# Eight feature tiles of the second modulation's shift rows, summed on VectorE in the latent stages

## The reference, cut to what matters

```python
def modulation(cond, w, b, n):
    m = jax.nn.silu(cond) @ w[:, :n * D_MODEL] + b[:n * D_MODEL]
    return jnp.split(m, n, axis=-1)          # shift, scale, gate

for i in range(DEPTH):                       # DEPTH = 2
    sh, sc, gt = modulation(c_lat, w_ada[i], b_ada[i], 3)
    u = x * (1.0 + sc) + sh
    y = even_mixer(u @ w_in_e[j], ...) if i == 0 else odd_mixer(u @ w_in_o[j], ...)
    x = layer_norm(alpha * x + gt * y, ln_g[i], ln_b[i])
```

## Time and profile before

| what | value |
|---|---|
| median of 3 runs | 2435.35 us (2435.2 to 2438.71) |
| the profiled execution's own time | 2434.28 us |
| its span, first to last instruction | 2432.4 us |
| mean granted TensorE clock | 0.993 of full |
| PE busy | 2355.5 us (97%) |
| DVE busy | 1436.6 us (59%) |
| ACT busy | 1081.7 us (44%) |
| POOL busy | 71.0 us (3%) |
| bytes moved by DMA | 492.88 MB, mean 203 GB/s |

### The profile page before, as it was taken

How to read it: one execution, slowest core, us unless ns; L and a number is a source line. 1 busy time by engine, 2 the same in 40 slices (tenths; PEclk the granted TensorE clock), 3 DMA queues, 4 the chain that set the end, 5 groups by cost and what they waited for, 6 DMA issues and landing times.

```text
span 2432.4 us, 29720 instructions
## 1 busy us (share of the span) xinstructions
PE 2355.5 (97%) x12180; PEld 1908.0 (78%) x12180; DVE 1436.6 (59%) x1400; ACT 1081.7 (44%) x1130; POOL 71.0 (3%) x116
## 2 busy tenths in 40 slices
PE   6999999999999999999999989999999999999998
PEld 2677887887687888878778777888888888888886
DVE  2354567566937786666567785655555545545454
ACT  2223645534744444546555443455544334334333
POOL 1000001000000000000000100000000000000000
PEclk9999999999999999999999999999999999999999
DMA  9974678757865796555545213654556566565563
GB/s 338 328 266 141 196 264 273 246 173 292 332 222 195 265 350 193 208 173 179 174 140 189 81 31 105 219 178 153 170 181 189 190 191 190 190 190 186 194 208 121
DMA packets 232163, 492.88 MB, mean 203 GB/s; under 512 B 21505, under 2 KB 23617, under 8 KB 224993
## 3 DMA queue, kind: packets, MB, share of 16 engines
q1 hardware_dynamic: 219792, 435.84, 54.6%
q0 software_dynamic: 12240, 55.18, 6.1%
HBM read 485.22 MB, written 5.77 MB: 202 GB/s over the span
## 4 chain that ended last, share of the span: by engine, by line
PE 87%; DVE 7%; ACT 2%; DMA 2%; issue 2%; SPq 0%; DVEq 0%; ACTq 0%
PE banks L2878 71%; PE banks L3011 5%; PE banks L2951 2%; DMA modulation_weights<-in_w_ada 1%; PE banks L2974 1%; DVE weights_lo L1671 1%; ACT weights_hi L842 1%; PE banks L3182 1%; PE banks L3051 1%; PE banks L3382 1%; PE banks L2991 1%; DMA weights_raw<-in_w_in_e 0%; DVE decayed_a L1961 0%; PE banks L3287 0%; DVE inverse_products L2583 0%
## 5 line engine op out<-in xcount | busy, mean ns | idle before, releaser
L1671 DVE TENSOR_TENSOR weights_lo<-weights_raw,weights_hi 128x2048 fp32r<-128x2048 f32 (+1 forms) x348 | 795.1, 2285 | 768.3 <-ACT weights_hi L842 766.8
L842 ACT ACTIVATE weights_hi<-weights_raw 128x2048 fp32r<-128x2048 f32 (+1 forms) x348 | 664.8, 1911 | 984.6 <-PE banks L2878 896.4
L2878 PE MATMUL banks<-weights_hi,acts_hi 128*128 128x512 f32 (+1 forms) x2032 | 797.9, 393 | 4.5 <-DVE weights_lo L1671 4.4
L2878 PE MATMUL banks<-weights_hi,acts_lo 128*128 128x512 f32 (+1 forms) x2032 | 789.4, 388 | 0.0
L2878 PE MATMUL banks<-weights_lo,acts_hi 128*128 128x512 f32 (+1 forms) x2032 | 789.1, 388 | 0.0
L2878 PEld LDWEIGHTS banks<-weights_hi,acts_hi 128*128 128x128 f32 x2032 | 381.5, 188 | 90.9 <-issue 15.0
L2878 PEld LDWEIGHTS banks<-weights_hi,acts_lo 128*128 128x128 f32 x2032 | 381.4, 188 | 78.9
L2878 PEld LDWEIGHTS banks<-weights_lo,acts_hi 128*128 128x128 f32 x2032 | 381.6, 188 | 76.1 <-issue 0.5
L2878 PE MATMUL banks<-weights_hi,hidden_hi 128*128 128x512 f32 x320 | 125.3, 392 | 0.5 <-DVE weights_lo L1671 0.5
L2878 PE MATMUL banks<-weights_hi,hidden_lo 128*128 128x512 f32 x320 | 124.6, 389 | 0.0
L2878 PE MATMUL banks<-weights_lo,hidden_hi 128*128 128x512 f32 x320 | 124.5, 389 | 0.0
(11 more groups left out here) (599 smaller groups left out, 2314.1 us busy)
## 6 DMA issues: line engine op xcount, KB each, us to landing
weights_raw<-in_w_in_e SPq DMA_DIRECT2D x72, 1024.0 KB, 5.5
weights_raw<-in_w_up SPq DMA_DIRECT2D x64, 1024.0 KB, 5.5
weights_raw<-in_w_down SPq DMA_DIRECT2D x64, 1024.0 KB, 5.1
weights_raw<-in_w_in SPq DMA_DIRECT2D x44, 1024.0 KB, 5.1
modulation_weights<-in_w_ada SPq DMA_DIRECT2D x64, 512.0 KB, 9.6
raw_eight<-in_w_ada SPq DMA_DIRECT2D x32, 1024.0 KB, 7.6
weights_raw<-in_w_in_o SPq DMA_DIRECT2D x32, 1024.0 KB, 5.6
gate_piece<-in_w_ada POOLq DMA_DIRECT2D x32, 512.0 KB, 5.5
```

The costliest lines, as they stand in the source:

```text
L842: eng.activation(WHI[:, c % 2, :, 0:n], RAW[:, sl, :, 0:n], ACT.Copy).then_inc(hi_ready, 1)
L1671: eng.tensor_tensor(WLO[:, c % 2, :, 0:n], RAW[:, c % 4, :, 0:n], WHI[:, c % 2, :, 0:n].bitcast(F32), ALU.subtract).then_inc(lo_ready, 1)
L2878: ins = eng.matmul(BANKS[:, par * 2 + h, 0:s.n], x[:, t, h * P:(h + 1) * P], w[:, c % 2, k, 0:s.n], start=(kc == 0 and k == 0 and m == 0), ...
```

## The change

Of the 16 feature tiles of the shift group, tiles 0 to 7 are summed on DVE, and tiles 8 to 15 and all 16 of the scale group stay with `plain_rows`. The list `PLAIN` has 24 chunks in place of 32, and the levels take one and two of them in turn.

- POOL loads 16 pieces of 0.5 MB (`row_piece`, three slots) after the latent decays are done, and DVE adds them into `row_sums_second` behind the chunks that `ROW_AT` names, chunks 14 to 26.
- PE adds the sums over the partitions to bank 0 in `summed_rows`, four matmuls with a stationary of ones, between `transposes("qT")` and `transposes("kT")`.
- `row_sums_second` takes the place at 111.5 KB where the parked keys were loaded to. The keys are now loaded to `latent_keys_again` at 103.5 KB, on POOL, behind a wait for the last `lat_q` chunk. `transposes("kT")` reads them there.
- The counts of the semaphores follow, and `second_gate` waits for the count that all pieces give.

```diff
+    ROW1 = place("row_ones", 68.6875, [P, 2])
+    GCH1 = [place(f"row_piece{k}", kb, [P, 2, NB]) for k, kb in enumerate((191.5, 195.5, 199.5))]
+    ROWS1 = place("row_sums_second", 111.5, [P, 4, NB])
+    LKR = place("latent_keys_again", 103.5, [P, 2, 2, NB])
...
+    ROW_PIECES = 16
+    ROW_TILES = ROW_PIECES // 2
+    PLAIN = [(0, kt) for kt in range(ROW_TILES, KT)] + [(1, kt) for kt in range(KT)]
+    ROW_AT = {14: 1, 15: 2, 16: 1, 17: 2, 18: 2, 19: 1, 20: 2, 22: 2, 24: 2, 26: 1}
...
 # SyncE
-                for m in range(s.kc * s.nblk):
+                for m, (grp, kt) in enumerate(PLAIN):
                     if m < 4:
                         eng.wait_ge(lo_ready, s.g0 - 3 + m)
                     elif m < 8:
                         eng.wait_ge(chunk_used, s.g0 + 2)
                     else:
                         eng.wait_ge(S("plain_used"), m - 7)
-                    eng.dma_start(RAW8[:, m % 8], s.view(m % s.kc, m // s.kc)).then_inc(cond_landed[m % 8], 16)
+                    eng.dma_start(RAW8[:, m % 8], s.view(kt, grp)).then_inc(cond_landed[m % 8], 16)
...
 # GpSimd
-        eng.wait_ge(S("ctx_kd"), 2)
-        eng.dma_start(NAT[:, 0:2, :, :].rearrange("p a b c -> p (a b c)"), lat_kept).then_inc(S("latent_kept"), 16)
...
+        bank_full(eng, J["lat_z"] + NJ["lat_z"] - 1)
+        eng.wait_ge(S("lat_la"), 2)
+        for i in range(ROW_PIECES):
+            m = GATE_PIECES + i
+            if i >= 3:
+                eng.wait_ge(S("gate_used"), m - 2)
+            eng.dma_start(GCH1[i % 3][:, :, :], ada1[i // 2 * P:(i // 2 + 1) * P, i % 2 * 1024:(i % 2 + 1) * 1024].rearrange(
+                "p (j n) -> p j n", n=NB)).then_inc(S(f"gate_landed{m % 3}"), 16)
+        eng.wait_ge(chunk_used, st["lat_q"].g0 + 8 + 2)
+        eng.dma_start(LKR[:, :, :, :].rearrange("p a b c -> p (a b c)"), lat_kept).then_inc(S("latent_kept"), 16)
         jobs_out(eng, "kT")
...
 # VectorE
+        def row_pieces(n):
+            def step():
+                for _ in range(n):
+                    m = pieces[0]
+                    pieces[0] += 1
+                    i = m - GATE_PIECES
+                    eng.wait_ge(S(f"gate_landed{m % 3}"), 16 * (m // 3 + 1))
+                    ch.wait()
+                    half = ROWS1[:, 2 * (i % 2):2 * (i % 2) + 2, :]
+                    if i < 2:
+                        ch.add(eng.tensor_scalar(half, GCH1[i % 3][:, :, :], CF[:, 0, 0:1], None, ALU.mult))
+                    else:
+                        ch.add(eng.scalar_tensor_tensor(out=half, in0=GCH1[i % 3][:, :, :], scalar=CF[:, i // 2, 0:1], in1=half,
+                                                        op0=ALU.mult, op1=ALU.add))
+                    ch.done("gate_used")
+            return step
...
-        lat_after = with_pieces(lat_after, LAT_PIECES)
+        lat_after = with_pieces(with_pieces(lat_after, LAT_PIECES), ROW_AT, row_pieces)
...
 # TensorE
+        def summed_rows():
+
+            eng.wait_ge(block_out, 2 * st["ada_plain"].b0 + 2)
+            eng.wait_ge(S("gate_used"), GATE_PIECES + ROW_PIECES)
+            for j in range(4):
+                eng.matmul(BANKS[32 * j:32 * j + 2, PLAIN_BANK[0], :], ROW1[:, :], ROWS1[:, j, :], start=True, stop=False)
...
         transposes("qT", lambda f, h: NAT[:, 4 + f // 4, h, (f % 4) * P:(f % 4 + 1) * P])
+        summed_rows()
         eng.wait_ge(S("latent_kept"), 32)
-        transposes("kT", lambda f, h: NAT[:, 0 + f // 4, h, (f % 4) * P:(f % 4 + 1) * P])
+        transposes("kT", lambda f, h: LKR[:, f // 4, h, (f % 4) * P:(f % 4 + 1) * P])
...
         for n, (d, l) in enumerate(LEVELS):
             Wn = DECAYED[n]
-            plain_rows(2 * n)
-            plain_rows(2 * n + 1)
+            for m in range(3 * n // 2, 3 * (n + 1) // 2):
+                plain_rows(m)
             eng.wait_ge(S("factors"), n + 1)
...
         def second_gate():
-            eng.wait_ge(S("gate_used"), KT)
+            eng.wait_ge(S("gate_used"), GATE_PIECES + ROW_PIECES + KT)
```

More of the change, by code:

```diff
@@ L527, in build @@
     COND_IN = 16 * 2 * KT // 4
-    FIRST_RANK_IN = COND_IN + 16 * (2 * KT // 8 + 1)
     PLAIN_BANK = (0, 2)
     GATE_PIECES = 2 * KT
-    GATE_IN = 16 * 11
+    ROW_PIECES = 16
+    ROW_TILES = ROW_PIECES // 2
+    PLAIN = [(0, kt) for kt in range(ROW_TILES, KT)] + [(1, kt) for kt in range(KT)]
+    PLAIN_END = [KT - ROW_TILES, len(PLAIN)]
+    GATE_IN = 16 * ((GATE_PIECES + ROW_PIECES) // 3)
     CTX_PIECES = {11: 1, 13: 1, 16: 2, 17: 2, 18: 2, 19: 2, 21: 2, 22: 1, 23: 2}
@@ L682, in _ @@
         eng.dma_start(CONST[:, 0:COMMON], a["common_consts"]).then_inc(S("consts_in"), 16)
+        eng.memset(ROW1[:, :], 1.0).then_inc(S("rank_steps"), 1)
         eng.memset(RT[:, :], 1.0).then_inc(S("rank_steps"), 1)
@@ L699, in _ @@
         eng.memset(RKR[:, :, :], 0.0).then_inc(S("rank_steps"), 1)
-        eng.wait_ge(S("rank_steps"), 2)
+        eng.wait_ge(S("rank_steps"), 3)
         for g in range(2):
@@ L953, in context_hi @@
             if q >= 2:
-                eng.wait_ge(S("rank_steps"), 4 + q - 1)
+                eng.wait_ge(S("rank_steps"), 5 + q - 1)
             eng.activation(CXH[:, q % 2], CR[:, :, :], ACT.Copy).then_inc(S("acts_hi"), 1)
@@ L1162, in plain_out @@
             s = st["ada_plain"]
-            eng.wait_ge(S("plain_used"), s.kc * (b + 1))
+            eng.wait_ge(S("plain_used"), PLAIN_END[b])
             for j in range(4):
@@ L1835, in rank_lo @@
         def rank_lo():
-            eng.wait_ge(S("rank_steps"), 3)
+            eng.wait_ge(S("rank_steps"), 4)
             eng.tensor_tensor(RKLO[:, :, :], RKR[:, :, :], RKHI[:, :, :].bitcast(F32), ALU.subtract)\
@@ L1935, in gate_pieces, with with_pieces @@
             return step
-        def with_pieces(after, at):
-            return {c: in_turn(*([after[c]] if c in after else []), *([gate_pieces(at[c])] if c in at else []))
+        def row_pieces(n):
[14 more added lines that the diff above has]
+            return step
+        def with_pieces(after, at, step=gate_pieces):
+            return {c: in_turn(*([after[c]] if c in after else []), *([step(at[c])] if c in at else []))
                     for c in sorted({*after, *at})}
@@ L2985, in rank_sums @@
             if q == 0:
-                eng.wait_ge(S("rank_steps"), 4)
+                eng.wait_ge(S("rank_steps"), 5)
                 bank_free(eng, jj)
@@ L3105, in plain_rows @@
             s = st["ada_plain"]
-            b, kt = m // KT, m % KT
-            if kt == 0:
+            b, kt = PLAIN[m]
+            if b == 1 and kt == 0:
                 eng.wait_ge(block_out, 2 * (s.b0 + b) + 2)
@@ L3111, in plain_rows @@
                 ins = eng.matmul(BANKS[32 * j:32 * j + 2, PLAIN_BANK[b], :], CF[:, kt, :], RAW8[:, m % 8, j, :],
-                                 start=(kt == 0), stop=(kt == KT - 1))
+                                 start=(b == 1 and kt == 0), stop=(kt == KT - 1))
             ins.then_inc(S("plain_used"), 1)
+        def summed_rows():
[3 more added lines that the diff above has]
+                eng.matmul(BANKS[32 * j:32 * j + 2, PLAIN_BANK[0], :], ROW1[:, :], ROWS1[:, j, :], start=True, stop=False)
         eng.wait_ge(block_out, 4 + 2 * st["ada_plain"].b0)
         transposes("qT", lambda f, h: NAT[:, 4 + f // 4, h, (f % 4) * P:(f % 4 + 1) * P])
+        summed_rows()
         eng.wait_ge(S("latent_kept"), 32)
-        transposes("kT", lambda f, h: NAT[:, 0 + f // 4, h, (f % 4) * P:(f % 4 + 1) * P])
+        transposes("kT", lambda f, h: LKR[:, f // 4, h, (f % 4) * P:(f % 4 + 1) * P])
         jobs_out(eng, "kT")
```

5 lines of the change are left out of this document (3 added, 2 removed).

## The result

The changed kernel takes 2446.88 us (median of 5 runs, 2445.95 to 2450.98), the kernel before beside it 2435.2 us (5 runs, 2432.48 to 2438.71): a ratio of 1.005, 95% interval 1.0035 to 1.0065. That is slower by 11.7 us, where +6.2 was forecast, and 0.4 us outside the range given. The profiled execution took 2447.01 (span 2445.2, mean granted clock 0.989; before 2434.28, 2432.4 and 0.993), so the two profiles differ by 12.8 us of span. I go through them in order of time.

What follows compares the result with a forecast made beforehand. PE carries most of the chain, but DVE sets the levels' end and `k_T` their start. +6.9 (keys) - 0.7 (level 0) + 0 (latent stages) = +6.2 us: 2440.5 profiled, 2441.5 by the median; range 2437.5 to 2446.5.

Steps and rivals of the forecast that it cites:

- The latent stages, 0: DVE's 16 added pieces hide in its idle time in the latent stages: 0, bounds 0 and +1.5 us.
- The levels, -0.7: Eight chunks fewer on PE remove only DVE's 0.74 us wait at level 0: -0.7 us.
- Rival 1: PE limits the levels, so 7.6 us come off and meet the +6.9: -0.7, 2434.6 us; chance 0.04.
- The keys' reload, +6.9: Before `kT`: reload lands at 579.9, transposes run at half clock, `k_T` is copied at 583.8 instead of 576.88: +6.9 us.
- The clock behind the change: After k's transposes: `diag` was to run at the full clock again; no later clock loss was counted.
- 2 (sharing): Reload shares the engines with SP's loads from 572.1, lands at 578.0: about +4, 2439.4 us; chance 0.12.
- 4 (behind more loads): Reload comes third or later behind SP's loads, landing 583.6 to 588: +10 to +14, 2445 to 2449 us; chance 0.12.
- 3: Reload goes ahead of SP's loads, lands at 575.3 without loss of clock: +0.6, 2436.0 us; chance 0.10.
- 5: A late first piece stalls the latent stages' stream by up to 1.5 us, on top of any other; chance 0.1.

Runs made afterwards that it cites:

- second measurement: The change unaltered, measured again beside the kernel before: 2446.06 us beside 2436.29, ratio 1.0043.
- filled_end: sums_after with three of the 24 row chunks kept for TensorE's wait before `gla_o`: 2434.49 us, ratio 1.0002 to the kernel before.
- late_only: The kernel before, all 32 chunks on TensorE, with only the keys' reload made late and moved to the change's place: 2445.8 us, ratio 1.0034.
- sp_held: The change, with the four SyncE chunk loads that start with the reload held until it has landed: 2441.91 us, ratio 1.0025.
- sp_first: The change, with the reload issued on SyncE's queue ahead of the four chunk loads: 2439.79 us, ratio 1.0013.
- early_keys: The change, with the keys reloaded before the last latent stage ends, in two 512 KB halves into places already free: 2440.24 us, ratio 1.001.
- sums_after: early_keys with the row sums behind k's transposes and GpSimd's bias loads released by the first used chunk: 2436.41 us, ratio 1.0004.

## Why the prediction was wrong

The direction was right, and the mechanism as far as it went: the keys come late, the clock falls in the wait, the levels return less than 1 us, the pieces are free. Two steps failed. The reload's term was too small by 1.1 us, and the prediction's "`diag` then runs at the full clock again" put everything that the clock does later at nothing. The second is the larger: of the 5.5 us between +6.2 and +11.7 (3.6 in the second measurement, +9.8) the path's terms explain 1.0, and 2.6 to 4.5 are left for the clock. In its own steps:

- **The latent stages, 0**: right; `lat_q` ends 0.23 late, and that was there before the first piece. The first piece was indeed the tightest: in filled_end VectorE waited 2.69 us for it and one `weights_lo` slipped by 0.45, but the stream had caught up by its last one.
- **The levels, -0.7**: right, -0.85 (83.04 against 83.89), by the wait at level 0 that went. Rival 1, TensorE as the limit, falls: with 7.6 us less work it waits 5.3 us for VectorE within the levels and 3.17 behind them.
- **The keys' reload, +6.9: this term was too small.** It measured +8.0, +8.2 and +8.4 (A of three profiles less 5.95). I had put the landing at 579.9, between one and two of SyncE's loads; it was 581.1. The issue was at 571.51, not 571.1, and after about one MB of the other queue the rest was shared and not served in turn, 9.6 us in all. The transposes at half clock took 3.30 us, where 3.2 was forecast. `k_T` was complete at 585.11 in place of the 583.8 forecast, and the landing is 1.2 of these 1.3 us.
- **The clock behind the change, put at nothing: this term failed, and it is the larger part.** I followed the clock to the end of k's transposes only. The half clock reached into `diag` in one of three profiles of the change, and the long fall in the delta rule's stage came in two of three. In the profiles the late falls are worth +5.4, +2.6 and +8.0 (B, C and D above 83.02, 10.63 and 1760.9), and in the two of before, with B at 83.89 in both, they are worth 0 and +1.7. That is the size of the difference between the path's +7.2 (8.0 - 0.85) and the +9.8 to +11.7 measured; that the medians differ by just these falls is inferred from five profiles and not shown. The fall in `gla_o` is in two of three profiles of the change and in one of two of before, so it explains 1.7 us of the first pair of profiles and little of the medians. The profile of before had the long fall too, shorter (within 1478 to 1486), and I had not read it there.
- **The rivals**: 2 (sharing) was half right, in what happens after 575; its time, 2439.4, was not. 4 (behind more loads) has the measured 2446.9 in its span of times by luck: the reload landed at 581.1, not at 583.6 or later. 3 did not happen. Nor did 5: the late first piece cost the stream nothing.

So late_only shows the cause of the loss in A, the reload's new time, sp_held and sp_first show that the other queue's loads make it as long as it is, and early_keys and sums_after show that the change can be had without it: the path is then 0.74 us shorter than before's (B 83.15, A 5.95). What is argued and not shown is why the falls far behind come more often with the versions of 24 chunks. That they do is in the runs and profiles, as far as the counts above go; whether by the shorter B, by the spacing of TensorE's short idle times in the levels or by something in the delta stage stays open. No version beats the kernel before: the best, filled_end, has 2434.49 and 2436.66 in two comparisons, beside 2436.21 and 2436.57, with ratios of 1.0002 (0.9993 to 1.001) and 1.0005 (0.9996 to 1.0014).

## What to carry to other kernels

Work taken off an engine that isn't the bound is worth only the wait that it caused, here 0.74 us of 7.6; look first at what the change must move to make room for it, here a 1 MB reload that had been 120 us early and became the last thing to arrive. When a trace is asked how two queues share, ask it at a place where both have more work waiting. A buffer that is free earlier, even in two halves, costs nothing and undoes it. And where TensorE's clock follows its idle times, a gain or loss of 1 us on the path can't be judged from a median of some ten runs: cut the profile into intervals, compare these, and look at the granted clock far behind the change too.

## What the runs showed of the hardware

- A transfer on GpSimd's queue that was issued 0.26 us after a 1024 KB load of SyncE (571.51 and 571.25) had its first packets 3.5 us later, when about one MB of the other queue had passed, and then got half of the engines (48.7% and 52.3%). With the other queue silent it began after 0.9 us and landed after 5.1 in place of 9.6.
- In the change's three profiles the clock was below full within 580 to 584, 578 to 586 and 580 to 592, after much the same idle time of TensorE (5.83, 5.96 and 5.87 us). What it costs depends on where it ends: inside the transposes 1.3 us, inside the scores behind them 2.3 to 2.6 more.
- Thrown-away transposes in a wait of 5.8 us took back 1.1 to 1.5 us in A; the median fell by 5.5.
- The clock also fell where TensorE had only short waits: in the levels (waits of 0.3 to 1.9 us) it was below full in stretches of some 4 to 8 us, in 11 of the 14 profiles with 24 chunks. At 45 us behind VectorE's start this cost 3.1 us, at 63 to 67 us nothing.
- The first multiply of a row piece (TENSOR_SCALAR, 128x1024) takes 0.75 us, the multiply and add (SCALAR_TENSOR_TENSOR) 1.28.
